# Attention and cross outputs computed with the values stationary, in a two-layer decoder trunk on one core

## The chip, the cores and the metric

One Trainium2 chip, one of its cores. The time is that of one execution of the whole program on the device, in microseconds (us), median over runs; the kernel before takes 2018.93 us. Five engines run side by side, each through its own list of instructions, and wait for each other by semaphores: PE (matrix products, its operand that is loaded first is called stationary, the one that streams is called moving), DVE (vector work), ACT (activations and copies), POOL, and SP, which here only starts DMAs. PE writes to PSUM, eight banks of 128 rows by 512 fp32 numbers.

## The reference

256 tokens, width 1024, two layers. Everything is fp32. Each layer:

```
h = RMSNorm(x);  proj = h @ w_in            # queries, keys, values, gates of all mixers
o_a = sliding-window attention, 8 heads of 64, 2 key/value heads, learned sinks
o_b = attention over the 64 keys that an indexer ranks highest, same shape
o_c = retention (4 heads);  o_d = causal pooling of four windows
x += (sum over a,b,c,d of sigmoid(gate_i) * (o_i @ w_branch_i)) @ w_out
x += CrossAttention(RMSNorm(x), RMSNorm(mem))   # 4 heads of 256, 256 memory tokens
x += SwiGLU(RMSNorm(x))    # layer 0: dense; layer 1: top 2 of 8 experts
```

and a last RMSNorm. In the attentions the part that matters is

```
p = exp(s - m);  p = p / (sum(p) + exp(sink - m))    # branch b and cross: without the sink
o = p @ v
```

## The kernel before

**Blocks of weights.** All large products go through `consume`: a block of 512 rows by 512 columns of a weight matrix is loaded by SP into one of six slots of `raw`; ACT copies it, rounded, to `w_hi` (L807); DVE writes the remainder, `raw - w_hi`, in place (L1254); PE then runs, for each of the two groups of 128 tokens, four k-tiles with three products each (L2016 to L2018), 24 products of 512 columns a block. The stationary side (`stat0`, `stat1`) is split in the same way into a high and a low part. ACT and DVE prepare a block five blocks ahead of PE.

**Order of the work.** `plan_chunks` lists the blocks of a layer: pu, idx, bq, kv, aq, rqk, rv, rg, then gate and up blocks of the branches D, C, A, B (`gateD0`, `gateD1`, `upD0` and so on; a gate is two blocks, an up one), then xkv, out, xq, xo. Each engine goes through that list and does its small work beside each block, by hand-written tables: `within` (between the two token groups of a block) and `after` on PE, `work` on ACT (before its high part of a later block), `work_of` on DVE (before its low part of a later block). What stands in an engine's table earlier is done earlier; a wait there holds all that follows on the engine.

**Small products.** They use PSUM banks 4 to 7 in rotation: `small_uses` is the list of uses, a use takes the bank of the fourth use before it, and `opened` waits until that one is emptied. The attention of a group g (a0, a1, b0, b1: branch and token group t) is a chain: `scores_of` on PE (two heads at a time, each on 64 of PE's 128 rows, L2069); `soft_start` on DVE (mask, row maximum); `exps` on ACT; `soft_end` on DVE (sum and its reciprocal `sinv`); `probs_of` on PE turns the unscaled probabilities by products with the identity (L2051), four tiles of 128x128 a bank; `probs_copied` on ACT; `outs_of` on PE, per head and key tile one product with the turned probabilities stationary and 64 columns of `v_ab` moving (L2089), 8(t+1) products; `soft_out` on DVE scales by `sinv` into `o_buf` (L1477). Before the up blocks of a branch `branch_t` turns `o_buf` (8 turns), and `split_rows` on ACT and DVE writes the high and low part to `stat1`.

**Cross attention.** The same chain in two halves i of two heads: `cross_scores`, `cross_start`, `cross_exps`, `cross_inv` (reciprocal), `cross_probs` (turn), `cross_outs` (L2191, probabilities stationary, 256 columns of values moving), `cross_out` (scale, L1551), `cross_rows` (8 turns a half), `split_pair` into `stat1`.

The transposes, one product of 128 columns each, are all recorded at L2051, and an fp32 product of the small kind is recorded as two instructions with a weight load each: the 48 products of a layer at L2089 are 96 records.

Of the kernel before, what the change touches and what calls it, by code (L numbers as in the profile page):

```python
# [27 lines left out]
ALU = mybir.AluOpType  # L28
# [100 lines left out]
def small_uses(layer):  # L129

    uses = ["h0", "h1", "h2", "h3"]
    if layer == 0:
# [14 lines left out]
def build(nc, x_in, mem_in, positions, norm_mix, w_in, attn_sink, w_branch, w_out, pool_w, pool_scale,  # L147
# [26 lines left out]
    with ctx:  # L174
# [142 lines left out]
        def small(layer, name):  # L317
# [11 lines left out]
        kv_landed = [sem(f"kv_landed{i}") for i in range(2)]  # L329
        hi_done = sem("hi_done")  # L330
# [4 lines left out]
                     for b in range(4)]  # L335
# [33 lines left out]
                              if g[0] == "a" else ["max", "shift", "inv"]) for g in GROUPS}  # L369
        soft_act = {g: Signal(sem(f"soft_act_{g}"), ["exp"] + (["sink exp"] if g[0] == "a" else [])) for g in GROUPS}  # L370
# [3 lines left out]
        xsoft_dve = Signal(sem("xsoft_dve"), [f"{s}{i}" for i in range(2) for s in ("max", "shift", "inv")])  # L374
# [186 lines left out]

        def f32_of(ap):
            return ap.bitcast(F32)
# [5 lines left out]
        def _(sp):  # L569
# [232 lines left out]
        def _(act):  # L802
# [12 lines left out]
            def hi_planned(n):  # L815
# [8 lines left out]
                if c.name == "kv":  # L824
                    act.wait_ge(kv_landed[i], (layer + 1) * 16)
                hi((0, n), c.n)
# [146 lines left out]
            def work(layer, name, i):  # L973
# [36 lines left out]
                elif at == ("rg", 1):  # L1010
                    probs_copied(layer, "a0")
                    evac(layer, CH["rg"], rg, rs_mix, ACT.Silu)
                elif at == ("gateD0", 0):
                    retention_sums(layer)
                elif at == ("gateD0", 1):
# [3 lines left out]
                elif at == ("gateD1", 1):  # L1019
                    gates_out(layer, "gateD1", "D0")  # L1020
                    act.wait_ge(small_full.sem, full_at(layer, "o_a0"))
                    act.wait_ge(weigh.sem, weigh.at(layer, "1 head3"))
                    probs_copied(layer, "a1")
                elif at == ("upD1", 0):
                    for t in range(NT):
                        split_rows(layer, f"tC{t}", stat1[:, 0, 4:8, :], t)
                elif at == ("gateC0", 1):
                    gates_out(layer, "gateC0", "D1")
                    exps(layer, "b0")
                    for t in range(NT):  # L1030
                        split_rows(layer, f"tA{t}", stat1[:, 0, 0:4, :], t)
                elif at == ("upC0", 0):
                    act.wait_ge(small_full.sem, full_at(layer, "o_a1"))
                    probs_copied(layer, "b0")
                elif at == ("gateC1", 1):
                    gates_out(layer, "gateC1", "C0")
# [6 lines left out]
                elif at == ("gateA1", 1):  # L1043
                    gates_out(layer, "gateA1", "A0")
                    for t in range(NT):
                        split_rows(layer, f"tB{t}", stat1[:, 0, 4:8, :], t)
# [203 lines left out]
        def _(dve):  # L1250
# [87 lines left out]

            def split_pair(layer, name, dst, q):
# [120 lines left out]
            def soft_end(layer, g):  # L1460
# [7 lines left out]
                dve.reciprocal(sinv[:, :], ssum[:, :]).then_inc(sig.sem, 1)  # L1468

            def soft_out(layer, g):  # L1470
                name = f"o_{g}"
                dve.wait_ge(soft_dve[g].sem, soft_dve[g].at(layer, "inv"))
# [3 lines left out]
                dst = o_buf[:, 1 if g[0] == "a" else 0, int(g[1]), :]  # L1476
# [68 lines left out]

            def cross_out(layer, i):
                dve.wait_ge(xsoft_dve.sem, xsoft_dve.at(layer, f"inv{i}"))
                for t in range(NT):
                    name = f"xo{t}{i}"
                    dve.wait_ge(small_full.sem, full_at(layer, name))  # L1550
                    (dve.tensor_tensor(  # L1551
                        tok[:, t, i * 512:(i + 1) * 512].rearrange("p (h n) -> p h n", h=2),
                        small(layer, name)[:, :].rearrange("p (h n) -> p h n", h=2),
                        sinv[:, 4 * t + 2 * i:4 * t + 2 * i + 2].rearrange("p (h a) -> p h a", a=1).broadcast_to([P, 2, T]),
                        ALU.mult)).then_inc(bank_sem(layer, name), 1)
# [6 lines left out]
            def work_of(layer, name, i):  # L1562
# [42 lines left out]
                elif at == ("gateD0", 0):  # L1605
                    soft_out(layer, "a0")
# [3 lines left out]
                elif at == ("upD0", 0):  # L1610
                    gated(layer, "upD0")
# [5 lines left out]
                elif at == ("upD1", 0):  # L1617
                    gated(layer, "upD1")
                    soft_out(layer, "a1")
                    for t in range(NT):  # L1620
                        split_rows(layer, f"tC{t}", 4, t)
                elif at == ("gateC0", 0):
                    soft_start(layer, "b0")
                    rank_rounds(layer, 1, 5, 6)
                elif at == ("gateC0", 1):
                    soft_end(layer, "b0")
                    for t in range(NT):
                        split_rows(layer, f"tA{t}", 0, t)
                elif at == ("upC0", 0):
                    gated(layer, "upC0")  # L1630
                    rank_rounds(layer, 1, 6, 7)
                elif at == ("gateC1", 0):
                    soft_out(layer, "b0")
# [11 lines left out]
                elif at == ("gateA1", 1):  # L1645
                    for t in range(NT):
# [947 lines left out]
```

## Time and profile before

| what | value |
|---|---|
| time of three runs, median (range) | 2018.93 us (2018.05 to 2020.81) |
| the profiled execution, its own time | 2019.58 us |
| its span | 2017.4 us |
| PE busy, share of the span | 1989.6 us, 99% |
| DVE busy | 1495.2 us, 74% |
| ACT busy | 1261.3 us, 63% |
| PE's granted clock, mean | 0.996 |

The span is what the profiler saw between the first and the last instruction; the time of an execution holds some 2 us around it. Times in a timeline count from the span's start. In a group of instructions "busy" is the union of their spans, and the spans of matrix products overlap, so their pitch (the distance from start to start) is what one costs.

### The profile page before, as it was taken

What the parts mean: (1) busy time and instruction counts of PE and PEld (TensorE: products, weight loads), DVE (VectorE), ACT (ScalarE), POOL (GpSimd) and SP (SyncE); (2) the same over time, 40 slices, a digit from 0 to 9 for tenths busy, and PEclk for the clock granted to TensorE, in tenths of its full rate; (3) what the DMA queues carried; (4) which work ended last, traced back from release to release, by engine and by line L of the source; (5) the groups of instructions that cost most, each with busy time, mean ns of one, the idle gap of its engine ahead of it and who ended that gap; (6) DMA issues with size and microseconds to landing.
All of it is one profiled execution on the core that took longest, in us unless ns stands there. A gap on an engine that the chain in (4) does not pass through costs nothing.

```text
span 2017.4 us, 25513 instructions
## 1 busy us (share of the span) xinstructions
PE 1989.6 (99%) x9465; PEld 1658.7 (82%) x9465; DVE 1495.2 (74%) x1384; ACT 1261.3 (63%) x1246; POOL 108.6 (5%) x166
## 2 busy tenths in 40 slices
PE   7999999999999999999999999999999999999998
PEld 6788888888888888888887888888888888888886
DVE  5776665455555776666449988888889889888998
ACT  6466545453433555645446777777767777776777
POOL 3300000000000210000000000000000000000130
PEclk9999999999999999999989999999999999999999
DMA  7444455355555544456458999999999999999994
GB/s 259 154 154 155 154 186 183 124 172 192 185 192 170 186 165 132 163 182 225 146 188 324 394 401 365 382 389 365 392 382 388 369 381 386 367 391 382 383 402 188
DMA packets 194811, 539.61 MB, mean 267 GB/s; under 512 B 10088, under 2 KB 17328, under 8 KB 194736
## 3 DMA queue, kind: packets, MB, share of 16 engines
q1 hardware_dynamic: 192288, 529.68, 72.1%
q0 software_dynamic: 2448, 8.91, 1.2%
q8 instruction: 50, 0.82, 0.2%
q14 instruction: 25, 0.20, 0.0%
HBM read 530.17 MB, written 8.39 MB: 267 GB/s over the span
## 4 chain that ended last, share of the span: by engine, by line
PE 93%; DVE 3%; ACT 1%; issue 1%; SPq 1%; DMA 1%; POOL 0%; DVEq 0%; ACTq 0%
PE bank L2423 14%; PE bank L2425 14%; PE bank L2424 14%; PE bank L2016 14%; PE bank L2018 14%; PE bank L2017 14%; PE bank L2051 2%; PE bank L2492 1%; PE bank L2089 1%; DVE expert_lo L1273 1%; PE bank L2172 1%; PE bank L2191 1%; PE bank L2069 1%; SPq L571 1%; ACT w_hi L807 1%
## 5 line engine op out<-in xcount | busy, mean ns | idle before, releaser
L813 ACT ACTIVATE w_hi<-raw 128x2048 fp32r<-128x2048 f32 x341 | 637.7, 1921 | 118.2 <-DMA raw<-in_moe_w_gu 82.8
L1273 DVE TENSOR_TENSOR expert_lo<-raw,w_hi 128x2048 fp32r<-128x2048 f32 x284 | 638.9, 2292 | 19.3 <-ACT w_hi L813 19.2
L2016 PE MATMUL bank<-w_hi,stat 128*128 128x512 f32 (+1 forms) x1296 | 511.3, 395 | 5.0 <-DVE low_in_place L1254 4.7
L2423 PE MATMUL bank<-w_hi,stat 128*128 128x512 f32 x1312 | 514.8, 392 | 1.5 <-DVE expert_lo L1273 1.4
L2425 PE MATMUL bank<-w_hi,stat 128*128 128x512 f32 x1312 | 511.1, 390 | 0.0
L1254 DVE TENSOR_TENSOR low_in_place<-raw,w_hi 128x2048 fp32r<-128x2048 f32 (+1 forms) x162 | 368.7, 2281 | 185.2 <-ACT w_hi L807 184.9
L2018 PE MATMUL bank<-w_hi,stat 128*128 128x512 f32 (+1 forms) x1296 | 503.3, 388 | 0.0
L2017 PE MATMUL bank<-low_in_place,stat 128*128 128x512 f32 (+1 forms) x1296 | 502.6, 388 | 0.0
L2424 PE MATMUL bank<-expert_lo,stat 128*128 128x512 f32 x1088 | 423.4, 389 | 0.0
L807 ACT ACTIVATE w_hi<-raw 128x2048 fp32r<-128x2048 f32 (+1 forms) x162 | 307.0, 1904 | 162.8 <-DMA raw<-in_dense_w_gu 57.9
L2016 PEld LDWEIGHTS bank<-w_hi,stat 128*128 128x128 f32 x1296 | 243.8, 188 | 56.2 <-issue 7.0
L2423 PEld LDWEIGHTS bank<-w_hi,stat 128*128 128x128 f32 x1312 | 246.3, 188 | 52.1 <-DVE expert_lo L1273 2.3
L2425 PEld LDWEIGHTS bank<-w_hi,stat 128*128 128x128 f32 x1312 | 246.2, 188 | 51.8
L2018 PEld LDWEIGHTS bank<-w_hi,stat 128*128 128x128 f32 x1296 | 243.5, 188 | 50.5
L2017 PEld LDWEIGHTS bank<-low_in_place,stat 128*128 128x128 f32 x1296 | 244.0, 188 | 47.3
L2424 PEld LDWEIGHTS bank<-expert_lo,stat 128*128 128x128 f32 x1088 | 204.3, 188 | 41.6
L1273 DVE TENSOR_TENSOR area_low<-raw,w_hi 128x2048 fp32r<-128x2048 f32 x56 | 130.2, 2324 | 0.3
L1785 DVE TENSOR_TENSOR stat<-bank,stat 128x512 fp32r<-128x512 f32 x56 | 36.4, 686 | 78.2 <-ACT stat L1181 78.2
L2424 PE MATMUL bank<-area_low,stat 128*128 128x512 f32 x224 | 87.2, 389 | 0.0
L1156 ACT ACTIVATE area<-bank 128x512 f32<-128x512 f32 x56 | 30.9, 596 | 87.1 <-PE bank L2425 86.9
L780 POOL COPY token_now<-slot_token 128x1 int32 x8 | 15.0, 1872 | 944.9 <-PE bank L2508 738.4
L2424 PEld LDWEIGHTS bank<-area_low,stat 128*128 128x128 f32 x224 | 42.1, 188 | 8.3
(304 smaller groups left out, 1257.6 us busy)
## 6 DMA issues: line engine op xcount, KB each, us to landing
raw<-in_moe_w_gu SPq DMA_DIRECT2D x224, 1024.0 KB, 7.9
raw<-in_moe_w_down SPq DMA_DIRECT2D x112, 1024.0 KB, 8.4
raw<-in_w_in SPq DMA_DIRECT2D x56, 1024.0 KB, 5.0
raw<-in_dense_w_gu SPq DMA_DIRECT2D x28, 1024.0 KB, 5.1
raw<-in_w_branch SPq DMA_DIRECT2D x16, 1024.0 KB, 5.1
raw<-in_w_xkv SPq DMA_DIRECT2D x16, 1024.0 KB, 5.1
raw<-in_dense_w_down SPq DMA_DIRECT2D x14, 1024.0 KB, 5.0
raw<-in_w_out SPq DMA_DIRECT2D x8, 1024.0 KB, 5.1
```

The costliest lines, as they stand in the source:

```text
L807: act.activation(w_hi[:, slot(b), :, 0:width], raw[:, slot(b), :, 0:width], ACT.Copy).then_inc(hi_done, 1)
L813: act.activation(expert_hi(b), expert_raw(b), ACT.Copy).then_inc(hi_done, 1)
L1254: dve.tensor_tensor(in_place_lo(b)[:, :, 0:width], raw[:, slot(b), :, 0:width], f32_of(w_hi[:, slot(b), :, 0:width]), ALU.subtract).then_i ...
L1273: dve.tensor_tensor(expert_low(b), expert_raw(b), f32_of(expert_hi(b)), ALU.subtract).then_inc(lo_done, 1)
L1785: ins = dve.tensor_tensor(expert_hid_t(1, v)[:, tiles, :], bank[4 + h][:, :].rearrange("p (k n) -> p k n", k=4), f32_of(expert_hid_t(0, v) ...
L2016: pe.matmul(dst, x_hi, wh, start=start, stop=False)
L2017: pe.matmul(dst, x_hi, wl, start=False, stop=False)
L2018: return pe.matmul(dst, x_lo, wh, start=False, stop=stop)
L2051: ins = pe.transpose(b[:, i * P:(i + 1) * P], src, ident[:, :])
L2423: pe.matmul(dst[:, :], x_hi, wh[:, at], start=start, stop=False)
L2424: pe.matmul(dst[:, :], x_hi, wl[:, at], start=False, stop=False)
L2425: ins = pe.matmul(dst[:, :], x_lo, wh[:, at], start=False, stop=stop)
```

## The change

The two operands of the output products change places. `outs_of` loads the values of one key/value head (128 keys by 64) as stationary and streams the turned probabilities of its four query heads (4 x 128 columns); the two key/value heads write to rows 0 to 63 and 64 to 127 of the bank. The output arrives turned, one column a token, so `branch_t` for A and B and its 8 turns each are gone. `cross_outs` does the same with 256 columns, so both `cross_rows` are gone. A turned output can't be scaled per token by `sinv`, so the probabilities are scaled before they are turned (in `soft_end` and `cross_inv`), and `probs_of` waits for that. The rows of the up weights of A and B are loaded in another order, by two DMAs of 64 partitions. `split_branch` reads the output from `o_buf`. In the tables the turns of a0, a1 and b0 stand one block later, their outputs too, the turns of a0 ahead of the retention outputs.

```diff
@@ small_uses
-             ... "p_a1_3", "o_a1", "tC0", "tC1", "s_b0_0", "s_b0_1", "tA0", "tA1",
+             ... "p_a1_3", "tC0", "tC1", "o_a1", "s_b0_0", "s_b0_1",
...
-             "xs00", "xs10", "xq2", "xq3", "xp00", "xp10", "xs01", "xs11", "xo00", "xo10", "xt0", "xt1",
-             "xp01", "xp11", "xo01", "xo11", "xt2", "xt3", "f0", "f1", "f2", "f3"]
+             "xs00", "xs10", "xq2", "xq3", "xp00", "xp10", "xs01", "xs11", "xt0", "xt1",
+             "xp01", "xp11", "xt2", "xt3", "f0", "f1", "f2", "f3"]
@@ SP, load_planned
+                elif c.name[:3] in ("upA", "upB"):
+                    branch, half = "ABCD".index(c.name[2]), int(c.name[3])
+                    rows = w_branch[layer, branch, :, half * 512:(half + 1) * 512].rearrange("(g m d) n -> g d m n", g=2, d=64)
+                    sp.wait_ge(block_used, number((0, n)) + 1)
+                    sp.dma_start(raw[0:64, n % SLOTS, :, :], rows[0]).then_inc(raw_landed[n % SLOTS], 16)
+                    sp.dma_start(raw[64:128, n % SLOTS, :, :], rows[1]).then_inc(up_landed[half], 16)
@@ ACT
+            def split_branch(layer, letter, k0, user):
+                act.wait_ge(bank_sem(layer, f"o_{letter.lower()}1"), emptied_at(layer, f"o_{letter.lower()}1"))
+                act.wait_ge(block_used, chunk_at(layer, user))
+                for t in range(NT):
+                    act.activation(stat1[:, 0, k0:k0 + 4, t * P:(t + 1) * P], branch_of(letter, t), ACT.Copy).then_inc(act_hi.sem, 1)
@@ ACT, work: probs_copied a0 from (rg, 1) to (gateD0, 0), behind retention_sums; a1 from (gateD1, 1)
@@ to (upD1, 0); b0 from (upC0, 0) to (gateC1, 0); split_branch A at (upC0, 0), B at (gateA1, 1)
                 elif at == ("gateC1", 1):
+                    copy_small(layer, "o_b0", o_buf[:, 0, 0, :].rearrange("p (k n) -> p k n", k=4), 4)
                     gates_out(layer, "gateC1", "C0")
@@ DVE, soft_end
                 dve.reciprocal(sinv[:, :], ssum[:, :]).then_inc(sig.sem, 1)
+                dve.wait_ge(sig.sem, sig.at(layer, "inv"))
+                nk = P * (int(g[1]) + 1)
+                dve.tensor_tensor(scores[:, :, 0:nk], scores[:, :, 0:nk],
+                                  sinv[:, :].rearrange("p (h a) -> p h a", a=1).broadcast_to([P, 8, nk]),
+                                  ALU.mult).then_inc(soft_normed, 1)
@@ DVE, soft_out
-                (dve.tensor_tensor(heads(dst, 8), heads(small(layer, name)[:, :], 8),
-                                          sinv[:, :].rearrange("p (h a) -> p h a", a=1).broadcast_to([P, 8, 64]),
-                                          ALU.mult)).then_inc(bank_sem(layer, name), 1)
+                dve.tensor_copy(o_buf[:, 1 if g[0] == "a" else 0, int(g[1]), :], small(layer, name)[:, :]).then_inc(bank_sem(layer, name), 1)
@@ DVE, work_of: soft_out a0 from (gateD0, 0) to (upD0, 0), a1 from (upD1, 0) to (gateC0, 0), b0 gone;
@@ cross_inv also scales the probabilities (2 x 128x512), cross_out gone; split_branch for A and B
@@ PE, probs_of
-                pe.wait_ge(soft_act[g].sem, soft_act[g].at(layer, "exp"))
+                pe.wait_ge(soft_normed, normed_at(layer, g))
@@ PE, outs_of
-                for h in range(8):
-                    for k in range(t + 1):
-                        ins = pe.matmul(b[:, h * 64:(h + 1) * 64], probs_t[:, h * (t + 1) + k, :],
-                                        v_ab[:, k, which, (h // 4) * 64:(h // 4) * 64 + 64], start=(k == 0), stop=(k == t))
+                for k in range(t + 1):
+                    for r in range(2):
+                        rows = slice(r * 64, r * 64 + 64)
+                        first = r * 4 * (t + 1) + k
+                        ins = pe.matmul(b[rows, :].rearrange("p (h n) -> p h n", h=4), v_ab[:, k, which, rows],
+                                        probs_t[:, first:first + 3 * (t + 1) + 1:t + 1, :], start=(k == 0), stop=(k == t))
@@ PE, cross_outs
+                for h in (2 * i, 2 * i + 1):
+                    b = opened(layer, f"xt{h}")
+                    for d in range(2):
                         for k in range(2):
...
+                            ins = pe.matmul(b[:, d * T:(d + 1) * T].rearrange("p (t n) -> p t n", t=NT),
+                                            v_tok[:, k, h * T + d * P:h * T + (d + 1) * P], x_probs_t[:, :, 2 * h + k, :],
+                                            start=(k == 0), stop=(k == 1))
@@ PE, after: probs_of a0 from (rg, 1) to (gateD0, 0) ahead of retention_outs, outs_of a0 to (gateD0, 1);
@@ probs_of a1 from (gateD1, 1) to (upD1, 0), outs_of a1 to (gateC0, 0) ahead of scores_of b0;
@@ probs_of b0 from (upC0, 0) to (gateC1, 0), outs_of b0 to (gateC1, 1) ahead of scores_of b1;
@@ branch_t A and B gone; cross_outs 0 from within (xkv3, 0) to after it; cross_rows 0 and 1 gone
```

## Rows read from the trace of the kernel before

**Rows 1.** The page: busy time (engine, us, share of the span, instructions).

```profile
PE 1989.6 (99%) x9465; PEld 1658.7 (82%) x9465; DVE 1495.2 (74%) x1384; ACT 1261.3 (63%) x1246; POOL 108.6 (5%) x166
```

**Rows 2.** What PE waited for (total us, times, longest), the longest behind the start.

```profile
PE bank L2016 <- DVE low_in_place L1254: 4.7, 1, 4.7
```

**Rows 3.** Stretches of layer 0: mixers from rg, and cross attention (us; busy of PE, weight loads, DVE, ACT, POOL; clock; DMA).

```profile
103.87:290.00 186.13, 186.13 (x973) 156.22 (x972) 123.53 (x151) 110.08 (x174) 0.00 (x0) 1.00 0.48 159
342.60:411.00 68.40, 68.40 (x331) 57.60 (x328) 31.30 (x31) 34.27 (x49) 0.00 (x0) 1.00 0.43 139
```

**Rows 4.** PE's groups by shape, PEld weight loads (count; busy us, mean ns; idle).

```profile
L2089 PE MATMUL bank<-v_ab,area 128*128 128x64 f32 x192 | 22.3, 273 | 0.0
...
L2089 PEld LDWEIGHTS bank<-v_ab,area 128*128 128x128 f32 x192 | 22.5, 192 | 0.5
...
L2051 PE MATMUL bank<-ident,tok 128*128 128x128 f32 x80 | 9.9, 272 | 0.0
...
L2051 PE MATMUL bank<-ident,o_buf 128*128 128x128 f32 x48 | 6.2, 273 | 0.0
```

**Rows 5.** PE's timeline about the outputs of b0 (start us, length us).

```profile
189.79 0.39 PE L2018 MATMUL bank<-w_hi,stat 128*128 128x512 f32 x1
190.02 1.89 PE L2089 MATMUL bank<-v_ab,area 128*128 128x64 f32 x16
191.72 0.48 PE L2016 MATMUL bank<-w_hi,stat 128*128 128x512 f32 x1
192.03 0.39 PE L2017 MATMUL bank<-low_in_place,stat 128*128 128x512 f32 x1
```

**Rows 6.** PE's timeline about the outputs of a1 and the turn of C.

```profile
160.72 3.68 PE L2089 MATMUL bank<-v_ab,area 128*128 128x64 f32 x32
164.23 1.04 PE L2051 MATMUL bank<-ident,o_buf 128*128 128x128 f32 x8
165.03 0.48 PE L2016 MATMUL bank<-w_hi,stat 128*128 128x512 f32 x1
```

**Rows 7.** PE's timeline about the turn of b0's probabilities.

```profile
183.69 1.03 PE L2051 MATMUL bank<-ident,area 128*128 128x128 f32 x8
184.48 0.48 PE L2016 MATMUL bank<-w_hi,stat 128*128 128x512 f32 x1
```

**Rows 8.** PE's timeline at the kernel's end: fp32 products of 512 columns.

```profile
2007.02 2.31 PE L2523 MATMUL bank<-heads_t 128*128 128x512 f32 x5
```

**Rows 9.** PE's timeline about the scores of b1, each on half of the rows.

```profile
197.06 0.39 PE L2018 MATMUL bank<-w_hi,stat 128*128 128x512 f32 x1
197.38 2.00 PE L2069 MATMUL bank<-heads_t 64*128 64x256 f32 x16
199.31 0.50 PE L2016 MATMUL bank<-w_hi,stat 128*128 128x512 f32 x1
199.65 0.40 PE L2017 MATMUL bank<-low_in_place,stat 128*128 128x512 f32 x1
```

**Rows 10.** DVE's timeline: before a1's scores, after its exponentials, after those of b1.

```profile
138.30 2.29 DVE L1254 TENSOR_TENSOR low_in_place<-raw,w_hi 128x2048 fp32r<-128x2048 f32 x1 [1.18 <-ACT w_hi L807]
140.71 1.29 DVE L1511 TENSOR_TENSOR tok<-bank,gate 128x512 f32<-128x512 f32 x2
...
155.77 0.20 DVE L1468 RECIPROCAL sinv<-ssum 128x8 f32<-128x8 f32 x1
...
211.90 0.20 DVE L1468 RECIPROCAL sinv<-ssum 128x8 f32<-128x8 f32 x1
```

**Rows 11.** PE's timeline: scores of a1, turn of b1's probabilities.

```profile
140.53 2.00 PE L2069 MATMUL bank<-heads_t 64*128 64x256 f32 x16
...
215.81 1.91 PE L2051 MATMUL bank<-ident,area 128*128 128x128 f32 x16
```

**Rows 12.** DVE's groups by shape: a product of 1024 numbers, and a scaling with broadcast.

```profile
L1515 DVE TENSOR_TENSOR tok<-tok,gate 128x1024 f32<-128x1024 f32 x12 | 14.7, 1225 | 0.4
...
L1477 DVE TENSOR_TENSOR o_buf<-bank,sinv 128x512 f32<-128x512 f32 x8 | 5.5, 690 | 11.4 <-PE bank L2089 11.4
```

More of the change, by code:

```diff
@@ L329, in build @@
         kv_landed = [sem(f"kv_landed{i}") for i in range(2)]
+        up_landed = [sem(f"up_landed{i}") for i in range(2)]
         hi_done = sem("hi_done")
@@ L560, in heads, with branch_of, normed_at @@
             return ap.rearrange("p (h d) -> p h d", h=n)
+        def branch_of(letter, t):
+            return o_buf[:, 1 if letter == "A" else 0, t, :].rearrange("p (k n) -> p k n", k=4)
+        def normed_at(layer, g):
+            return layer * len(GROUPS) + GROUPS.index(g) + 1
         def f32_of(ap):
@@ L825, in hi_planned @@
                     act.wait_ge(kv_landed[i], (layer + 1) * 16)
+                if c.name[:3] in ("upA", "upB"):
+                    act.wait_ge(up_landed[int(c.name[3])], (2 * layer + "AB".index(c.name[2]) + 1) * 16)
                 hi((0, n), c.n)
@@ L1029, in work @@
                     exps(layer, "b0")
-                    for t in range(NT):
-                        split_rows(layer, f"tA{t}", stat1[:, 0, 0:4, :], t)
                 elif at == ("upC0", 0):
+                    split_branch(layer, "A", 0, "upD1")
+                elif at == ("gateC1", 0):
                     act.wait_ge(small_full.sem, full_at(layer, "o_a1"))
@@ L1044, in work @@
                     gates_out(layer, "gateA1", "A0")
-                    for t in range(NT):
-                        split_rows(layer, f"tB{t}", stat1[:, 0, 4:8, :], t)
+                    split_branch(layer, "B", 4, "upC1")
                 elif at == ("upA1", 0):
@@ L1544, in cross_inv @@
                 dve.reciprocal(of_heads(sinv, i), of_heads(ssum, i)).then_inc(xsoft_dve.sem, 1)
-            def cross_out(layer, i):
                 dve.wait_ge(xsoft_dve.sem, xsoft_dve.at(layer, f"inv{i}"))
                 for t in range(NT):
[L1549 to L1555, printed above, removed]
+                    probs = xs_scores[:, t, 2 * i:2 * i + 2, :]
+                    ins = dve.tensor_tensor(probs, probs, sinv[:, 4 * t + 2 * i:4 * t + 2 * i + 2].rearrange(
+                        "p (h a) -> p h a", a=1).broadcast_to([P, 2, T]), ALU.mult)
+                ins.then_inc(xsoft_dve.sem, 1)
             def keys(layer, q):
@@ L1610, in work_of @@
                 elif at == ("upD0", 0):
+                    soft_out(layer, "a0")
                     gated(layer, "upD0")
@@ L1622, in work_of @@
                 elif at == ("gateC0", 0):
+                    soft_out(layer, "a1")
                     soft_start(layer, "b0")
@@ L1626, in work_of @@
                     soft_end(layer, "b0")
-                    for t in range(NT):
-                        split_rows(layer, f"tA{t}", 0, t)
                 elif at == ("upC0", 0):
                     gated(layer, "upC0")
+                    split_branch(layer, "A", 0)
                     rank_rounds(layer, 1, 6, 7)
                 elif at == ("gateC1", 0):
-                    soft_out(layer, "b0")
                     rank_rounds(layer, 1, 7, 8)
@@ L1645, in work_of @@
                 elif at == ("gateA1", 1):
-                    for t in range(NT):
-                        split_rows(layer, f"tB{t}", 4, t)
+                    split_branch(layer, "B", 4)
                 elif at == ("upA1", 0):
@@ L2176, in cross_probs @@
             def cross_probs(layer, i):
-                for t in range(NT):
-                    emptied(layer, f"xs{t}{i}")
+                pe.wait_ge(xsoft_dve.sem, xsoft_dve.at(layer, f"normed{i}"))
                 for t in range(NT):
@@ L2213, in within @@
                 at = (name, i)
-                if at == ("xkv3", 0):
-                    cross_outs(layer, 0)
-                elif at == ("xkv3", 1):
-                    cross_rows(layer, 0)
+                if at == ("xkv3", 1):
                     cross_probs(layer, 1)
@@ L2263, in after @@
                     scores_of(layer, "a1")
-                elif at == ("gateD1", 1):
+                elif at == ("upD1", 0):
                     probs_of(layer, "a1")
-                elif at == ("upD1", 0):
-                    outs_of(layer, "a1")
                     emptied(layer, "ro0")
@@ L2325, in after @@
                     cross_scores(layer, 1)
+                elif at == ("xkv3", 0):
+                    cross_outs(layer, 0)
                 elif at == ("xo1", 1) and layer:
@@ L2351, in ready @@
                     emptied(layer, needs[name, i])
+                elif name in ("upA0", "upB0"):
+                    pe.wait_ge(branch_split.sem, branch_split.at(layer, name[2]))
                 elif name == "xkv0":
```

58 lines of the change are left out of this document (21 added, 37 removed), and 4 rows, old and new, of the table uses.

## Prediction

> **What bounds the kernel now.** I read the page first: PE is busy for 99% of the span, DVE for 74% and ACT for 63% [rows 1]. Because spans of matrix products overlap, that 99% alone doesn't prove a bound. So I went to the view of waits next: behind the first microseconds the longest time that PE stands is one wait of 4.7 us for DVE [rows 2], and in the two stretches of layer 0 that the change touches PE has no gap at all, at a granted clock of 1.00 (2.4 GHz), while DVE is busy for 66% and ACT for 59% of the first, and for less of the second [rows 3]. There the kernel is as long as PE's list of instructions. A microsecond taken out of that list is a microsecond of the kernel, as long as nothing that is moved arrives late; work added to DVE or ACT costs nothing until PE waits for it.
>
> The weight blocks have a long lead: the low part that DVE writes at 138.30 [rows 10] is of the block that PE starts at 165.03 [rows 6], 24 us after it is done. The attention chains have none such, and there I looked for new waits.
>
> **What the turns cost.** Eight turns take 184.48 - 183.69 = 0.79 us, and the large product behind a stretch of small ones comes 0.31 after its first instead of 0.23 [rows 5, 7], 0.08 more: 0.88 us for a set of eight. Gone per layer: a set each for A and B and two in the cross attention. The counts bear it out: 32 of 48 turns from `o_buf` and 32 of 80 from `tok` [rows 4]. 4 x 0.88 = 3.5 us a layer.
>
> **What the output products cost.** Before, a block with t = 0 is 16 records in 191.72 - 190.02 = 1.70 us, with the 0.08 1.78 us [rows 5]; with t = 1 it is 32 records in 164.23 - 160.72 = 3.51, 3.59 us [rows 6]. That is 0.107 us a record for only 64 columns. After, t = 0 is 4 records of 512 columns and t = 1 is 8. The trace has such fp32 products at its end: five in 2.31 us, the last 0.59 long, so (2.31 - 0.59) / 4 = 0.43 us a record [rows 8]. Column by column that is twice the old work: the pair fills the array's two halves in turn. The gain hangs on whether the two halves of a pair run at once. The trace before has no product with 64 output rows. The nearest row is the scores' pair, which share PE by halves of the rows: 16 records of 256 columns leave 199.31 - 197.06 - 0.23 = 2.02 us between large products, 2.13 with the late one behind them (0.34 instead of 0.23) [rows 9]. At half of 0.43 each, eight after each other would be 1.72 and sixteen 3.44. So two do run at once, at a cost of 0.41 us for going into that mode and out.
>
> Bounds of a new output block: together, 2 x 0.43 + 0.41 = 1.27 (t = 0) and 4 x 0.43 + 0.41 = 2.13 (t = 1); one after the other, 2.13 and 3.85. I take "together", since the scores' row is the nearest and a pair here is as independent: other output rows, other values. Saved: 0.51 and 1.46, for two branches 3.9 us a layer. One after the other it would be a loss of 0.35 and 0.26, 1.2 us a layer.
>
> The cross outputs stay at 8 products of 256 columns for each half, only stationary and moving swap: no change.
>
> **What is added elsewhere.** DVE multiplies the probabilities: 1.23 us for 1024 numbers [rows 12], 2.29 for 2048, by the row of a low part [rows 10], so 7.0 us a layer; a scaling with broadcast costs no more per number (0.69 for 512) [rows 12]. It lies in a stretch where DVE has 62 us free [rows 3]. The cross probabilities, the copies in `soft_out` and the splits from `o_buf` take the place of operations of the same 512 numbers. The up weights of A and B come by two DMAs of 64 partitions; the lead of 24 us hides them, even at twice their time. If that cover were gone, ACT would stand at `w_hi` and PE at the block.
>
> **Where a moved step may be late.** I followed the three engines' lists from the changed block on (layer 0; layer 1 repeats it). The turns of a0 now stand behind gateD0's first block, 5.4 us later, and find their probabilities ready: these come only 1.2 us later than before.
>
> 1. The last bank of a1's scores is the bank of o_a0, which DVE now empties only in (upD0, 0). DVE is at its low part until 140.59 [rows 10], its copy of 0.69 is done at about 141.2. PE comes to a1's scores 0.4 us earlier than at 140.53 [rows 11], to its second pair of banks 1.0 later, at 141.0. A wait of 0.25 us.
> 2. The same copy moves a1's softmax back by 0.45: its reciprocal comes at 156.5 instead of 155.97, the scaled probabilities at 158.8. PE ended upD1 at 160.72 [rows 6] with a1's 16 turns ahead of it; without them (1.7 us, as those of b1 [rows 11]) and with 0.2 left of its lead it ends at 158.8. A wait of 0 to 0.2. Behind it stand C's turns and the retention up blocks.
> 3. b1: up to here a0, a1, b0 and the turns of A have saved 0.51 + 1.46 + 0.51 + 0.88 = 3.4 us and the waits cost 0.4, so PE is 3.0 earlier than at 215.81 [rows 11], at 212.8. DVE, on which this softmax hangs, is only some 1.3 earlier: the reciprocal that began at 211.90 [rows 10] ends at 210.8, the scaled probabilities come at 213.1. A wait of 0.3.
>
> Together some 0.5 us a layer; what is later gets more room from each. The turns of b0, the outputs and the up blocks of A and B find their operands 2 us or more early. In the cross attention the longest step, scores of half 1 to scaled probabilities, has the whole of xkv3's first block, 5.4 us and more. The split of A, at upC0, is five blocks ahead of upA0.
>
> **Sum.** 3.5 + 3.9 - 0.5 = 6.9 us a layer, 13.8 in both. The profiled execution took 2019.58 us, so 2005.8; it lies 0.65 above the median of the runs, 2018.93, and I forecast a median of 2005.1 us.
>
> **A rule against the change.** The rows show that a full-width weight load passes beneath a running product: large products follow each other at 0.23 us with a load before each, the loads busy for 156 of 186 us [rows 3, 5]. The Trainium skill (TensorE: Matmul & The Clock Gate, Part 3: Packing small matmuls, The mechanism) says that loads overlap running products only when the row groups differ; two halves of the columns share all row groups. Read strictly, this gives the second rival; the trace of large products disagrees with the strict reading. The same page's table reports 2.38 times for three column tiles, which speaks for "together"; no run shown here has column tiles.
>
> **Rivals.**
>
> - *The pairs run one after the other.* For it: no row shows halves of columns. Against it: the scores' pairs. 3.5 - 1.2 = 2.3 us a layer, no waits, 4.6 in all: 2014.3 us.
> - *The pairs run one after the other and their weight loads aren't hidden.* 24 records a layer with a load each; the old products' loads took 0.19 us [rows 4]. That is 4.6 us a layer more: 2.3 - 4.6 = -2.3, 4.6 slower: 2023.5 us. It decides from 0.10 us a record (2.3 / 24). Against it: the old products of 64 columns follow each other at 0.107 us, less than one load.
> - *PE waits for the scaled probabilities.* The pairs run together, but DVE, held by a low part that waits for ACT, comes late at the three places by another microsecond each. For it: DVE stood 1.18 us for ACT before such a part [rows 10]. 3 us a layer: 2011 us; with half of it 2008.
> - *The gain is given back elsewhere*, to the DMAs or the experts. Against it: PE has no wait of that kind now [rows 2]. 2018.9 us.
>
> **Chances.** Forecast 0.67 (2003 to 2007), late probabilities 0.11, one after the other 0.13, weight loads 0.05, given back 0.04. A measurement of this kernel tells 0.2% (4 us) from no change. The rival with 2014.3 lies just beyond that bound; I count two thirds of it as faster. Faster 0.67 + 0.11 + 0.08 = 0.86, less a little for what I have not seen: 0.84; same 0.09; slower 0.07. The range: its low end is no wait at all (14.8 saved: 2004.1) and 0.5 us less in each layer for stretches that merge (outputs with the scores behind them enter the mode once), 2003.0; its high end takes in the pairs one after the other, 2014.5.
>
> **What would show it.** The records of the outputs: 12 products, 24 records a layer, in pairs some ns apart every 0.43 us, a t = 1 block 2.1 us from large product to large product. If they start each 0.43 us after the one before, the first rival holds; at 0.6, the second. The turns from `o_buf` fall to 16, those from `tok` to 48. PE's idle rows should name `bank` for DVE (scaled probabilities, o_a0's copy) with under 1.5 us in all. The mixers of layer 0 from rg to 290 should be about 5 us shorter, the cross attention 1.8. The forecast fails if a wait of more than 1 us stands before a1's or b1's turns.

## The result

The changed kernel takes 2003.08 us (median of 4 runs, 2002.82 to 2003.28), the kernel before in the same session 2019.16 us (4 runs, 2018.05 to 2020.81): 16.1 us less. The ratio on record is 0.9918, with a 95% interval of 0.9906 to 0.9929, which puts the gain between 14 and 19 us. The forecast was 2005.1 us, a gain of 13.8. The median lies at the low end of the range (2003.0), and the ratio, taken of 2018.93, gives 2002.4, just below it.

The profiled execution took 2003.19 us, its span 2000.9; before these were 2019.58 and 2017.4. First the page of the changed kernel, its line of busy time, which answers to [rows 1]:

```profile
PE 1973.6 (99%) x9257; PEld 1633.1 (82%) x9257; DVE 1507.2 (75%) x1390; ACT 1263.7 (63%) x1248; POOL 109.7 (5%) x166
```

PE is busy for 16.0 us less, about the whole gain; DVE has 12 us more. PE's waits (what waits, what it waits for: total us, times, longest):

```profile
PE bank L2547 <- DMA area<-in_pool_scale: 7.4, 1, 7.4
PE bank L2042 <- DVE low_in_place L1280: 4.7, 1, 4.7
...
PE bank L2077 <- POOL gate L752: 1.5, 1, 1.5
```

No row names the scaled probabilities (L1506) or the copy of o_a0 (L1515); the waits of up to 0.2 us that are read below show only in the distances between starts. The groups by shape, which answer to [rows 4]:

```profile
L2117 PE MATMUL bank<-area,v_ab 128*64 128x512 f32 x48 | 12.1, 609 | 0.0
...
L2077 PE MATMUL bank<-ident,tok 128*128 128x128 f32 x48 | 5.7, 272 | 0.0
...
L2077 PE MATMUL bank<-ident,o_buf 128*128 128x128 f32 x16 | 2.1, 272 | 0.0
```

192 records of output products have become 48, 32 turns from `o_buf` and 32 from `tok` are gone, as forecast. And the timeline of PE about a0's outputs, then a1's with the scores of b0 behind them, then b1's turns and b1's outputs (start us, length us; the answers to [rows 5, 6, 11]):

```profile
133.07 0.39 PE L2044 MATMUL bank<-w_hi,stat 128*128 128x512 f32 x1
133.39 1.08 PE L2117 MATMUL bank<-area,v_ab 128*64 128x512 f32 x4
134.40 0.50 PE L2042 MATMUL bank<-w_hi,stat 128*128 128x512 f32 x1
...
166.55 0.39 PE L2044 MATMUL bank<-w_hi,stat 128*128 128x512 f32 x1
166.86 1.94 PE L2117 MATMUL bank<-area,v_ab 128*64 128x512 f32 x8
168.73 1.16 PE L2095 MATMUL bank<-heads_t 64*128 64x128 f32 x16
169.82 0.50 PE L2042 MATMUL bank<-w_hi,stat 128*128 128x512 f32 x1
...
212.12 1.95 PE L2077 MATMUL bank<-ident,area 128*128 128x128 f32 x16
213.83 0.48 PE L2042 MATMUL bank<-w_hi,stat 128*128 128x512 f32 x1
...
219.15 0.39 PE L2044 MATMUL bank<-w_hi,stat 128*128 128x512 f32 x1
219.47 1.94 PE L2117 MATMUL bank<-area,v_ab 128*64 128x512 f32 x8
221.34 0.50 PE L2042 MATMUL bank<-w_hi,stat 128*128 128x512 f32 x1
```

The eight records of b1's outputs start in four pairs, at 219.47, 219.95, 220.38 and 220.81, the two of a pair 0.007 us apart. So the two halves of the columns run at once, as far as starts can tell; the experiment without halves below tests it.

What a stretch of small products costs PE net is read in one way throughout: from the start of the last large product before it to the start of the fifth large product behind it, less five times 0.227 us, the distance at which large products follow each other. The layer then sums up as follows (us, layer 0; layer 1 differs by some hundredths in each line):

| stretch | before | after | saved | forecast |
|---|---|---|---|---|
| turns of A, B; two sets of the cross attention | 4 x 0.89 | 0 | 3.55 | 3.5 |
| a0: turns, retention outputs, outputs | 0.90 + 4.49 | 3.58 + 1.23 | 0.58 | 0.51 |
| a1: turns, outputs, turns of C, scores of b0 | 1.77 + 4.42 + 1.31 | 2.65 + 3.18 | 1.67 | 1.46 |
| b0: turns, outputs, scores of b1 | 0.89 + 1.81 + 2.16 | 0.90 + 3.16 | 0.80 | 0.51 |
| b1: outputs | 3.60 | 2.10 | 1.50 | 1.46 |
| waits: scores of a1 (2.16 to 2.34), turns of b1 (1.78 to 1.81) | | | -0.21 | -0.5 |
| a layer | | | 7.9 | 6.9 |

Two layers make 15.8 us of the span's 16.4. Four landmarks in PE's list agree with this: the turns ahead of a0's scores (the start of the mixers), the turns of the merged branches (`tok`, the end of the mixers), and two sets of turns of `x` behind the cross attention. This is the kernel before:

```profile
103.88 1.03 PE L2051 MATMUL bank<-ident,gate 128*128 128x128 f32 x8
...
281.96 1.91 PE L2051 MATMUL bank<-ident,tok 128*128 128x128 f32 x16
...
407.30 1.04 PE L2051 MATMUL bank<-ident,x 128*128 128x128 f32 x8
...
417.10 1.03 PE L2051 MATMUL bank<-ident,x 128*128 128x128 f32 x8
```

and this the changed one:

```profile
104.01 1.03 PE L2077 MATMUL bank<-ident,gate 128*128 128x128 f32 x8
...
275.92 1.91 PE L2077 MATMUL bank<-ident,tok 128*128 128x128 f32 x16
...
399.47 1.03 PE L2077 MATMUL bank<-ident,x 128*128 128x128 f32 x8
...
408.53 1.04 PE L2077 MATMUL bank<-ident,x 128*128 128x128 f32 x8
```

The mixers went from 178.08 to 171.91, 6.17 us; the cross attention from 125.34 to 123.55, 1.79 us. The last stretch, from one set of turns of `x` to the next, went from 9.80 to 9.06, 0.7 us that no part of the change explains.

### The profile page after: what moved, and what is told of

The parts are those of the page before. It is cut to its first block, busy times and chain, and to the rows that moved or that the text cites. A ratio compares the mean times of both kernels' runs of the same rounds, so it can differ in the third digit from the quotient of the medians.

```text
span 2000.9 us, 25101 instructions
## 1 busy us (share of the span) xinstructions
PE 1973.6 (99%) x9257; PEld 1633.1 (82%) x9257; DVE 1507.2 (75%) x1390; ACT 1263.7 (63%) x1248; POOL 109.7 (5%) x166
## 4 chain that ended last, share of the span: by engine, by line
PE 93%; DVE 3%; ACT 1%; issue 1%; SPq 1%; DMA 0%; POOL 0%; DVEq 0%; ACTq 0%
PE bank L2435 14%; PE bank L2437 14%; PE bank L2436 14%; PE bank L2042 14%; PE bank L2044 14%; PE bank L2043 14%; PE bank L2077 2%; PE bank L2504 1%; DVE expert_lo L1299 1%; PE bank L2200 1%; PE bank L2218 1%; PE bank L2095 1%; SPq L582 1%; PE bank L2117 1%; ACT w_hi L824 0%
## 5 line engine op out<-in xcount | busy, mean ns | idle before, releaser
L2042 PEld LDWEIGHTS bank<-w_hi,stat 128*128 128x128 f32 x1296 | 243.7, 188 | 58.8 <-issue 10.3
```

Of the source, the lines that this page charges most:

```text
L2042: pe.matmul(dst, x_hi, wh, start=start, stop=False)
```

## The experiments

**Each half alone.** Two kernels. `cross_only` is the kernel before with `cross_inv` scaling the probabilities, `cross_probs` waiting for that, `cross_outs` with the values stationary, and `cross_out` and `cross_rows` gone. `attention_only` is the changed kernel with all of these as before.

> The kernel before with the cross attention's part of the change alone: probabilities scaled before their turn, outputs with the values stationary, the two cross_rows gone. My theory: the change is a plain sum on PE's list, and this part is two sets of eight turns a layer, 1.77 us as the two traces show (cross turns of 1.78 and 0.89 us become 0.90 and 0). 3.5 us in both layers: about 2015.5. Also open: the 0.67 us that the changed kernel saves at the start of the dense layer, which neither part names. If it follows from the cross attention ending otherwise on ACT or DVE, this run has it too: 2014.9, and PE's stand of 0.37 us before the first dense block is gone from its trace. Rival: scaling the cross probabilities costs DVE time that PE waits for, and the gain of this part alone is under 2 us (over 2017).

> The changed kernel with the cross attention as in the kernel before. My theory: turns of A and B gone (1.78 us a layer), outputs of the four groups shorter by 0.58, 1.67, 0.80 and 1.50 us as the two traces show (4.55), waits 0.2: 6.1 us a layer, 12.3 in all, plus 0.67 if the start of the dense layer belongs to this part: 2006.9, or 2006.2 with it. With the run of the cross part alone the gains add up to the whole change (16.1 us). Rival: the parts are not independent, for instance because the saved time of the mixers lets DMAs come late or early in the cross attention; then the sum of the two parts misses the whole by over 1.5 us.

Measured: 2015.23 and 2007.70 us, against 2019.42 for the kernel before on that chip (ratios 0.9979, interval 0.9969 to 0.9989, and 0.9939, interval 0.9923 to 0.9956): 4.2 and 11.7 us, together 15.9 where the whole gave 16.1. The parts add up to the whole within the noise of the runs (each interval is 4 to 7 us wide), and the traces say the same: in the first the cross turns read 0.90 and 0 net and the mixers' stretches are those of the kernel before, in the second the mixers' stretches are those of the changed kernel within 0.02.

**The kernel before, profiled again.** Each part alone also had a short last stretch, 9.06 and 9.08 us, so it hangs on neither part. Either the kernel before is slow there or its one trace is.

> The kernel before, unchanged, for a second trace. The question is the 0.37 us that PE stood before the first dense block of the kernel before, behind a load that took 6.2 us to land, and that no changed variant has shown. Theory: it is one load's luck in one execution; then this trace does not have it, or has it elsewhere. Rival: it belongs to the order of the work before; then it stands there again, at about 411.5 us, and the changed kernel gains it in truth.

This execution took 2018.89 us, its span 2016.6. The same two turns of `x`:

```profile
407.08 1.04 PE L2051 MATMUL bank<-ident,x 128*128 128x128 f32 x8
...
416.23 1.03 PE L2051 MATMUL bank<-ident,x 128*128 128x128 f32 x8
```

9.15 us, and no stand of PE for `stat`. So 0.65 us of that stretch belong to the one execution that was profiled first, and they make up most of the 0.71 by which the spans of the two executions differ (2017.35 and 2016.64). That a late load caused it is likely but not shown. The change does not gain it: against this second trace the span of the changed kernel is 15.7 us shorter, and the table has 15.8.

**No halves.** Are the output products cheap because two of them share the array? Here each takes the full width; the outputs are then sums over both halves of the heads.

```diff
-                        ins = pe.matmul(b[rows, :]..., v_ab[:, k, which, rows],
-                                        probs_t[...], start=(k == 0), stop=(k == t))
+                        ins = pe.matmul(b[:, :]..., v_ab[:, k, which, 0:P],
+                                        probs_t[...], start=(k == 0 and r == 0), stop=(k == t and r == 1))
```

> The changed kernel, but the output products of the attentions take both key/value heads' values (128 columns) as stationary and write all 128 rows of the bank; the products of both halves are added up in it, so this computes the sum of two heads' groups in place of each. As many products of the same length, only that none is half an array wide. My theory (two halves of the columns run at once, at some 0.4 us for entering and leaving that mode): a block becomes 4 x 0.43 + 0.08 = 1.80 us for t = 0 and 8 x 0.43 + 0.08 = 3.52 for t = 1; a0 loses 0.57, a1 with the scores of b0 3.52 + 1.31 - 0.08 - 3.18 = 1.57, b0 with the scores of b1 1.80 + 2.16 - 0.08 - 3.16 = 0.72, b1 1.42: 4.3 us a layer, 8.6 in all, 2011.7. Rival (the pairs do not overlap, the products of 64 columns are cheap for another reason, such as a shorter weight load): no change, 2003.

Measured 2010.88 us (ratio to the kernel before 0.9953, interval 0.9937 to 0.9970), 7.8 more than the changed kernel, where 8.6 was expected. PE about b1's outputs in this kernel, and its group by shape with the weight loads:

```profile
221.43 0.39 PE L2044 MATMUL bank<-w_hi,stat 128*128 128x512 f32 x1
221.66 3.59 PE L2116 MATMUL bank<-area,v_ab 128*128 128x512 f32 x8
224.69 0.79 PE L2042 MATMUL bank<-w_hi,stat 128*128 128x512 f32 x1
```

```profile
L2116 PE MATMUL bank<-area,v_ab 128*128 128x512 f32 x48 | 21.9, 592 | 0.0
L2116 PEld LDWEIGHTS bank<-area,v_ab 128*128 128x128 f32 x48 | 9.1, 189 | 8.3 <-issue 7.7
```

Net 1.74 us for a0 and 3.45 for b1, 4.74 for a1 with b0's scores, 3.86 for b0 with b1's: 4.1 us a layer more, less the 0.18 of a1's wait, which is gone since PE comes later. The records follow each other at 0.428 us although each has a weight load of 189 ns before it: loads are hidden beneath a running fp32 product even at full width and over all rows. So the second rival's price was zero, and pairing is worth 3.9 us a layer, half of the gain. It also shows what doesn't merge: full-width outputs with b0's scores right behind them cost 4.74, and apart they would cost 3.45 + 1.31 = 4.76.

**The order in the queue.** With the pairs shown, must their two products be neighbours?

```diff
-                for k in range(t + 1):
-                    for r in range(2):
+                for r in range(2):
+                    for k in range(t + 1):
```

> The changed kernel with the two loops of the output products exchanged: first both key tiles of the one key/value head, then both of the other. Blocks with t = 0 are as they were; in the blocks with t = 1 only the middle one of three neighbourhoods is between different halves of the columns. Theory A (only neighbours in the queue run at once): 8 records at 0.43, less one overlap, plus 0.41 for the mode: 3.4 us instead of 2.10 for b1 and as much more for a1, 2.6 us a layer, 5.2 in all: 2008.3. Theory B (PE looks past products for the same half, or pairs something else than neighbours): no change, 2003.1.

Measured 2003.35 us. b1's outputs:

```profile
219.29 1.95 PE L2117 MATMUL bank<-area,v_ab 128*64 128x512 f32 x8
221.16 0.50 PE L2042 MATMUL bank<-w_hi,stat 128*128 128x512 f32 x1
```

Still 1.95 us in four pairs, only that the two of a pair start 0.013 us apart. Theory A has fallen: with two products (four records) of one half queued before the first of the other, both halves still run together. The trace does not label the halves; this is read from the length, which would be 3.4 us one after the other. How far PE can reach ahead was not tried.

**Stretches that merge.** The scores of b0 half a block later, so that large products stand between them and a1's outputs:

```diff
@@ PE, after (gateC0, 0)
                     outs_of(layer, "a1")
-                    scores_of(layer, "b0")
@@ PE, within (gateC0, 1)
+                    scores_of(layer, "b0")
```

> The changed kernel, but the scores of b0 stand half a block later, between the two token groups of gateC0's second block, instead of right behind the outputs of a1. My theory (products that share the array are entered and left once for a whole stretch): the two stretches cost 2.10 and 1.31 us instead of 3.18 together, 0.23 us a layer more, 0.5 in all: 2003.6, visible only in the trace. Rival: the merged stretch is cheap because of the place, not because of the neighbourhood; then the two add up to 3.18.

Measured 2003.34 us. The timeline of the two stretches:

```profile
166.04 0.39 PE L2044 MATMUL bank<-w_hi,stat 128*128 128x512 f32 x1
166.35 1.94 PE L2117 MATMUL bank<-area,v_ab 128*64 128x512 f32 x8
168.22 0.51 PE L2042 MATMUL bank<-w_hi,stat 128*128 128x512 f32 x1
...
170.89 0.39 PE L2044 MATMUL bank<-w_hi,stat 128*128 128x512 f32 x1
171.21 1.16 PE L2095 MATMUL bank<-heads_t 64*128 64x128 f32 x16
172.30 0.50 PE L2042 MATMUL bank<-w_hi,stat 128*128 128x512 f32 x1
```

Net 2.10 and 1.31, 3.41 against 3.18 in one: 0.23 us for one more way in and out. The outputs use halves of the columns and the scores halves of the rows, and going from the one to the other costs less than going out and in again. Since the full-width outputs of the experiment before saved only 0.02 in the same place, the 0.23 belongs to the halves and not to stretches being neighbours. Before the change, the scores' stretch stood alone and the old outputs needed no mode; now two of four output blocks share it with the scores behind them.

**The two places without room.** a1's turns in their old place:

```diff
@@ PE, after; ACT, work
+                elif at == ("gateD1", 1): probs_of(layer, "a1")       # ACT: probs_copied(layer, "a1")
                 elif at == ("upD1", 0):
-                    probs_of(layer, "a1")                             # ACT: probs_copied(layer, "a1")
```

> The changed kernel, but the turns of a1's probabilities and their copies by ACT stand where the kernel before had them, behind gateD1's second block, one block earlier. My theory (the changed kernel needs the later place because the scaling on DVE comes between): PE is through with that block at about 153.9 us in layer 0 and the scaled probabilities come at 158.5, so PE stands 4.6 us a layer for DVE; nothing later gives it back. 9.2 us in all, 2012.3, and the waits of PE name DVE L1506. Rival: PE's lead is given back later, because DVE sets the pace of the chain up to b1 anyhow; then under 5 us in all, below 2008.

Measured 2018.09 us, nearly the whole gain lost (ratio to the kernel before 0.9991, interval 0.9981 to 1.0001). PE's timeline:

```profile
158.28 3.53 PE L2077 MATMUL bank<-ident,area 128*128 128x128 f32 x16 [5.17 <-DVE area L1506]
161.57 0.47 PE L2042 MATMUL bank<-w_hi,stat 128*128 128x512 f32 x1
```

A stand is a time in which PE does nothing because it waits. This one is 5.17 us, near the 4.6 expected, but the total missed the expected 2012.3 by 5.8 us: behind the stand the 16 turns take 3.53 us instead of 1.91. Net, the stretch of these turns reads 8.72 us in layer 0 and 9.56 in layer 1 (stand 5.12) against 1.81 for such turns without one: 14.7 of the 15.0 us, of which the stands are 10.3. The windows of that kernel show why (window us: length; busy PE, PEld, DVE, ACT, POOL; granted clock; DMA share, GB/s). In layer 0 the granted clock is 0.50 (1.2 GHz) while the turns run and 1.00 (2.4 GHz) after:

```profile
155.00:158.20 3.20, 0.00 (x0) 0.00 (x0) 3.13 (x4) 0.83 (x2) 0.00 (x0) 0.99 0.75 284
158.20:161.50 3.30, 3.22 (x15) 3.22 (x16) 0.02 (x1) 1.56 (x3) 0.00 (x0) 0.50 0.02 5
161.50:165.00 3.50, 3.50 (x18) 2.91 (x17) 0.72 (x1) 2.63 (x3) 0.00 (x0) 1.00 0.00 0
```

In layer 1 it is 0.50 from 783.9 to 787.3 and 0.58 from there to 790.0. An estimate from these windows, the length times the part of the clock that is missing, is 1.7 us lost in layer 0 and 2.8 in layer 1; the stretches cost 1.7 and 2.6 us more than their stands.

**Late probabilities.** What if DVE had been slower at every group? Here it multiplies the probabilities twice.

```diff
                                   ALU.mult).then_inc(soft_normed, 1)
+                dve.wait_ge(soft_normed, normed_at(layer, g) - 1)
+                dve.tensor_tensor(scores[:, :, 0:nk], scores[:, :, 0:nk], sinv[...], ALU.mult).then_inc(soft_normed, 1)
```

> The changed kernel with the scaling of the probabilities in soft_end done twice, one after the other (the attention's probabilities are multiplied by the reciprocal of their sum twice, so its outputs are other numbers). It prices the rival of late probabilities. My theory: a0 has 3 us of room and hides its extra 1.2; a1 has 0.2 us of room and b1 none, each gets 2.3 us more, so PE stands some 2.1 us before a1's turns and, since a1's delay moves the scores of b1 by as much, 2.2 us before b1's: 4.3 us a layer, 8.6 in all, 2011.7, if a stand costs its own length. The run with a1's turns in their old place lost 1.7 us more than its stand of 5.2, at a granted clock of 0.74 to 0.81 about the turns; if a stand of 2 us does that too, up to 1.7 more for each of four stands: up to 2018. Rival (the scaling is far off the critical path): under 2 us in all, 2005.

Measured 2018.23 us, the upper end of what was expected. PE's waits have one new row; below it stands the timeline of a1's and b1's turns in layer 0, and of both in layer 1:

```profile
PE bank L2081 <- DVE area L1510: 10.1, 4, 3.0
```

```profile
160.64 1.97 PE L2081 MATMUL bank<-ident,area 128*128 128x128 f32 x16 [2.05 <-DVE area L1510]
...
217.28 3.61 PE L2081 MATMUL bank<-ident,area 128*128 128x128 f32 x16 [2.98 <-DVE area L1510]
...
786.39 2.84 PE L2081 MATMUL bank<-ident,area 128*128 128x128 f32 x16 [2.05 <-DVE area L1510]
...
844.68 3.09 PE L2081 MATMUL bank<-ident,area 128*128 128x128 f32 x16 [2.98 <-DVE area L1510]
```

The stands are 2.05 and 2.98 us a layer, 10.1 in all, and net the four stretches cost 2.26, 4.80, 3.92 and 4.79 us more: 15.8, against the 15.1 measured. One stand of 2.05 cost 2.26, about its length; the same stand in layer 1, and both of 2.98, cost 1.8 to 1.9 us more than their length, with the granted clock down behind them (0.50 from 217.3 to 219.9 in layer 0; in layer 1 0.68 from 786.4 to 789 and 0.52 to 790.8 behind a1's stand, 0.76 from 844 to 846.6 and 0.50 to 848 behind b1's). Behind the cheap stand it stayed at 1.00 (160.6 to 163.2). What decides between the two stands of 2.05 us is open. The rival with late probabilities priced each stand at its own length; for stands of 2 us and more that was too low in three cases of four, and shorter ones were not tried.

**The scaling left out.**

```diff
-                dve.tensor_tensor(scores[:, :, 0:nk], scores[:, :, 0:nk], sinv[...], ALU.mult).then_inc(soft_normed, 1)
+                dve.tensor_copy(ses[:, :], sinv[:, :]).then_inc(soft_normed, 1)
```

> The changed kernel without the scaling of the attention's probabilities (they go on as exp values, so the attention's outputs are not normalised; DVE signals with a copy of 8 numbers instead). Theory: the scaling is work of 7.0 us a layer that DVE has room for; PE waits for it by 0.03 us at b1 and not at a1, so nothing is gained: 2003.0, within 0.3 us of the changed kernel. Rival: the scaling's time on DVE delays low parts and costs PE elsewhere; then 2001 or less, and the gain of the change is smaller than PE's list says.

The total, 2120.98 us, says nothing of DVE, because this kernel does more expert work: the accumulation of the experts' results is 63 operations here and 56 in the changed kernel, and the experts' products are an eighth more. The outputs aren't normalised, so the router sees other numbers. Ahead of the router the question can still be read. The stretch from the first to the second landmark in layer 0 is

```profile
103.67 1.03 PE L2075 MATMUL bank<-ident,gate 128*128 128x128 f32 x8
...
275.47 1.91 PE L2075 MATMUL bank<-ident,tok 128*128 128x128 f32 x16
```

171.80 us against 171.91, and in layer 1 171.87 against 171.95. The 7 us of scaling on DVE cost PE 0.1 us a layer.

**The copy earlier.** The one wait that is left and can be mended:

```diff
@@ DVE, work_of (gateD0, 1)
+                    soft_out(layer, "a0")
                     retention_normed(layer)
                 elif at == ("upD0", 0):
-                    soft_out(layer, "a0")
```

> The changed kernel with DVE's copy of o_a0 one place earlier, ahead of the retention's scaling, so before the low part that now stands between it and a1's scores. My theory: PE's wait for the bank before a1's scores (0.18 us in layer 0, 0.22 in layer 1: 2.34 and 2.38 us for that stretch against 2.16 before) goes, nothing else moves on PE, since the retention's scaling has 20 us to the turn of C. 0.4 us in all: 2002.7, not to be told from 2003.1 by the times, but the stretch should read 2.16 in the trace. Rival: the 0.2 us is no wait for the copy but the cost of entering the mode for halves of the rows behind other work; then the stretch stays at 2.34.

Measured 2003.12 us (5 runs; ratio to the kernel before 0.9920, interval 0.9906 to 0.9933), the same time. a1's scores read 2.16 net in both layers, so the 0.2 was the wait for the copy; but the stretch of a1's turns went from 2.65 to 2.74 in layer 0 and from 2.64 to 2.78 in layer 1. PE now comes at 157.86, the scaled probabilities at 157.85:

```profile
155.56 2.29 DVE L1506 TENSOR_TENSOR area<-area,sinv 128x2048 f32<-128x2048 f32 x1
```

Half or more of what the first wait gave back is taken by the next one in the chain. No version was measurably better than the changed kernel.

## Why the prediction came out as it did

- **What bounds the kernel** was right: PE's list became 16.0 us shorter and the kernel 16.1 to 16.4.
- **The turns**, 3.5 us a layer: 3.55. Right.
- **The pairs run at once**: right, and shown by the experiment without halves. The block costs of 1.27 and 2.13 us were measured as 1.23 and 2.10. The first rival (one after the other, 2014.3) and the second (weight loads not hidden) are out. The experiment came to 2010.9 and not to 2014.3 because the rival counted 0.41 us of mode in each of the eight blocks, 3.3 us, and products at full width have no mode to enter.
- **The step that failed** is the sum's term for the outputs, "3.9 us a layer", which measured 4.55. The mechanism was right and the size was off: the term priced each block as if it stood alone. The prediction knew of "0.5 us less in each layer for stretches that merge", but put it into the low end of the range instead of the sum. a1's and b0's outputs stand ahead of scores that go through the mode anyway: 0.23 us each, 0.46 a layer, shown for a1 by parting them, read from the table for b0 (1.23 + 2.16 - 3.16). With this and some 0.04 for each block the outputs saved 0.6 us a layer more than forecast.
- **The waits**, 0.5 us a layer, were the second term mis-sized: 0.21. The copy of o_a0 cost 0.18 and 0.22 (forecast 0.25). a1's turns found their operands 0.2 us early (forecast 0 to 0.2 of wait); its reciprocal began 0.17 us later than before (155.94 against 155.77) and not 0.45. At b1, forecast 0.3, it was 0.03: PE came 3.7 us earlier than before (forecast 3.0) but the reciprocal of b1 2.4 earlier (it began at 209.53 instead of 211.90) where the prediction had 1.3. The last time that DVE stands for PE on the way to it is at b0's scores; from there only its own list and ACT hold it. This is DVE there before,

```profile
171.97 1.29 DVE L1443 TENSOR_TENSOR area<-bank,sel_mask 128x512 f32<-128x512 f32 x2 [1.88 <-PE bank L2069]
```

and in the changed kernel:

```profile
170.02 1.29 DVE L1478 TENSOR_TENSOR area<-bank,sel_mask 128x512 f32<-128x512 f32 x2 [0.48 <-PE bank L2095]
```

It starts 1.95 us earlier, about what a0's and a1's stretches saved up to there (0.58 + 1.67, less the wait of 0.18). The other 0.4 us of the 2.4 arose in the lists of DVE and ACT, which no run takes apart.

- Together 0.6 + 0.3 and what is left of rounding, a microsecond a layer, 2.0 us in all: that is 2005.1 against 2003.1. The step from the profiled execution to the median (0.65 us) was right, and the second trace of the kernel before shows where in the span it lay.
- **Added work on DVE costs nothing**: right, 0.1 us a layer for 7 us of work. **The two DMAs of half the partitions** take 6.1 us each to land (median of 16) instead of 5.1 for the one before (median of the 16 blocks of all branches), and since the second lands last, a block is there 7.5 to 7.9 us after the first was issued. ACT does stand for them; its waits for the up weights before and after are

```profile
ACT w_hi L807 <- DMA raw<-in_w_branch: 13.7, 7, 4.5
```

```profile
ACT w_hi L824 <- DMA raw<-in_w_branch: 27.1, 8, 6.9
```

but PE has no wait for a block in those stretches. The lead of the blocks hid the delay, as the prediction said.

## What to carry to other kernels

Where the list of one engine is the time, count what an edit removes from that list, and price products by what stands next to them: here two small products on different halves of the array took the time of one, and stretches that use halves were cheaper next to each other. Scaling the probabilities instead of the output moves work ahead of the turn in the chain; it is free only if the turn moves back by as much, and here a place one block too early lost 15.0 of the 16.1 us. Room of 0.0 to 0.2 us before a turn is no margin: in three of four cases a stand of 2 to 3 us cost 1.6 to 1.9 times its length.

## What the hardware did that was not expected

- A stand of PE has a price beyond its length. Stands of 2.98 us (twice), 5.17 and 5.12 us and one of 2.05 us were followed by a lower granted clock during the products behind them, down to 0.50 (1.2 GHz), and cost 1.7 to 2.6 us more than their length; the other stand of 2.05 us was followed by a clock of 1.00 and cost 0.2 more.
- Products for different halves of the columns start together (0.007 us apart), and still do so where four records of the one half stand in the queue before the first of the other (0.013 us apart).
- Fp32 products of 512 columns follow each other at 0.428 us with a full-width weight load of 189 ns before each. The Trainium skill (TensorE: Matmul & The Clock Gate, Part 3: Packing small matmuls, The mechanism) has loads overlap running products only when the row groups differ, and names a background weight buffer as the other way for a load to go ahead; these rows show loads hidden with all row groups shared, so the first sentence alone would mislead.
- Products on halves of the columns with products on halves of the rows right behind them cost 0.23 us less than with large products between (3.18 against 3.41). Full-width products in place of the first saved 0.02 (4.74 against 4.76).
